# A mixture-of-experts trunk: where the kept expert rows are weighted and added, VectorE or GpSimd

## Chip, core and metric

The kernel runs on one core of a Trainium2 chip. The metric is device time in microseconds for one execution of the whole program; lower is better.

## What is computed

Two decoder layers on 256 tokens of width 1024 in fp32, then a final RMSNorm. The second layer ends in a mixture of eight SwiGLU experts, of which each token uses two. That part matters here:

```python
def _moe(x, router, wg, wu, wd):
    logits = (x @ router).astype(jnp.float32)
    top_val, top_idx = lax.top_k(logits, TOP_K)
    top_w = jax.nn.softmax(top_val, axis=-1)
    gate = jnp.sum(jax.nn.one_hot(top_idx, N_EXPERTS, dtype=jnp.float32) * top_w[..., None], axis=-2)
    y = jnp.zeros_like(x)
    for e in range(N_EXPERTS):
        y = y + gate[..., e:e + 1].astype(x.dtype) * _swiglu(x, wg[e], wu[e], wd[e])
    return y
```

D_MODEL is 1024, an expert is 3584 wide, and the result is added to the residual `h`.

## The kernel before

Every engine has its own program, written out by hand; semaphores join them. There is no scheduler: each engine runs its instructions in the order of the code.

**Weights.** A product in fp32 is made of three matmuls on parts of the operands. A weight tile of 2 MB lies in one of seven ring slots (`ring_a`, `ring_b`) and is taken in four quanta of 128x1024. For each quantum ScalarE copies it, rounded, to `w_hi` (L806), VectorE subtracts to get the rest, `w_lo` (L1416), and TensorE runs six matmuls on it (`three`, L1546 to L1548). `w_hi` and `w_lo` have four slots (NQ), so ScalarE and VectorE can be at most four quanta ahead of TensorE: a slot is refilled when TensorE signals `q_used`. VectorE's L1416 reads two SBUF operands, a ring slot and `w_hi`.

**Experts.** The loop over experts ("items" 0 to 7) has seven blocks f of 512 hidden columns. Each block takes a gate tile, an up tile and a down tile, so an item has 84 quanta. Beside them VectorE does two things for a block, both with one operand in PSUM: the product of the activated gate with up, called `mul` below (L1485), and the rest of the transposed hidden block, `hT_lo` (L1474). TensorE transposes the hidden block at L2067.

**Kept rows.** Tokens are gathered by expert. The outputs of experts 0 to 6 are stored in DRAM rows `xs`. While the last expert (item 7) runs, GpSimd's queue gathers each token's stored rows back with indirect DMAs into `tokens` (128 x 2 x 1024): first the one choice (n=0, two DMAs, t=0 and 1), later the other (n=1). `gate_kept`, worked out in `kept_gates` at the beginning of the expert stage, holds their weights. VectorE adds weight times row to `h` in four instructions (`kept_rows`, L1435), one behind the `mul` of each of the blocks f = 3, 4, 5 and 6. The second gather overwrites `tokens`, so it waits for the first two additions (`kept_added`).

**End.** Behind the last quanta TensorE scatters the last expert's rows (L2125, L2126), VectorE adds them to `h` (L1450), and the final norm and two stores of the output follow.

Of the kernel before, what the change touches and what calls it, by code (L numbers as in the profile page):

```python
# [11 lines left out]
ALU = mybir.AluOpType  # L12
ACT = mybir.ActivationFunctionType
AX = mybir.AxisListType
# [4 lines left out]
T = S // P  # L19
# [10 lines left out]
NE, FE = 8, 3584  # L30
# [59 lines left out]
def trunk(nc, A, consts_d, bands_d, out):  # L90
# [64 lines left out]
    AHEAD = 2 * NQ  # L155
# [4 lines left out]
    fills, n = {}, 0  # L160
# [5 lines left out]
    GCOLS, n = {}, 0  # L166
# [14 lines left out]
    with ExitStack() as ctx:  # L181
# [3 lines left out]
        def sem(name):  # L185
            return ctx.enter_context(nc.semaphore(name))
# [5 lines left out]
        h = sbuf("h", [T, D])  # L192
# [11 lines left out]
        tokens = sbuf("tokens", [T, D])  # L204
# [8 lines left out]
        gate_kept = sbuf("gate_kept", [T, 2])  # L213
# [51 lines left out]
        valid = sbuf("valid", [T, ITEMS], on=route)  # L265
# [38 lines left out]
        def slot(s):  # L304
# [26 lines left out]
            "logits_done", "top_done", "top_exp", "sel_done", "routed"))  # L331
        rwg_done = sem("rwg_done")
        xn_done = sem("xn_done")
        zeroed, xs_cleared, rows_done, xs_in, xg_loaded = map(sem, (
            "zeroed", "xs_cleared", "rows_done", "xs_in", "xg_loaded"))
        y_out, y_stored, kept_in, kept_added = map(sem, ("y_out", "y_stored", "kept_in", "kept_added"))
# [109 lines left out]
        @block.gpsimd  # L446
        def _(pool):
            def gains(*parts):
                at = 0
                for v, w in parts:  # L450
                    pool.dma_start(gain[:, at:at + w], v.partition_broadcast(P)).then_inc(gain_in, 16)
                    at += w
            pool.wait_ge(loaded[0], 16)
            pool.dma_start(sgu_w[:, :, :], A["sgu_w"][0].rearrange("g p q -> p g q")).then_inc(even_in, 16)
            gains((A["sgu_ln_g"][0], 512), (A["sgu_ln_b"][0], 512))
            for n, v in enumerate(("lam_q1", "lam_k1", "lam_q2", "lam_k2")):
                pool.dma_start(lamv[:, n, :], A[v][0].partition_broadcast(P)).then_inc(even_in, 16)
            with nc.allow_non_contiguous_dma("512 words, once"):
                pool.dma_start(sgu_b[:, :], A["sgu_b"][0].rearrange("g p -> p g")).then_inc(even_in, 16)
            pool.dma_start(rw[:, :, :], A["router"][0].rearrange("(c p) n -> p c n", p=P)).then_inc(rw_in, 16)  # L460

            pool.wait_ge(even_in, 16 * 6)
            pool.affine_select(out=sgu_w[:, :, :], in_=sgu_w[:, :, :], compare_op=ALU.is_ge, fill=0.0, base=0,
                               pattern=[[0, 4], [-1, P]], channel_multiplier=1).then_inc(sgu_masked, 1)

            pool.wait_ge(gain_in, 16 * 2)
            pool.wait_ge(ln_ready, 1)
            for t in range(T):
                vg = proj[:, t, 2048:2560]
                pool.tensor_scalar(vg, vg, st("ROOT", t, 1), st("LNBIAS", t, 1), ALU.mult, ALU.add).then_inc(ln_step, 1)  # L470
                pool.wait_ge(ln_step, 2 * t + 1)
                pool.tensor_tensor(vg, vg, gain[:, 0:512], ALU.mult).then_inc(ln_step, 1)
                pool.wait_ge(ln_step, 2 * t + 2)
                pool.tensor_tensor(vg, vg, gain[:, 512:1024], ALU.add).then_inc(ln_applied, 1)
            pool.wait_ge(ln_applied, 2)
            gains((A["norm_ffn_odd"][0], D))
            pool.wait_ge(h_done, 2)
            pool.memset(zeros[:, :], 0.0).then_inc(zeroed, 1)
            pool.dma_start(bands, bands_d).then_inc(bands_in, 16)
            pool.dma_start(pool_w[:, :, :], A["pool_w"][0].rearrange("g c d -> c g d")).then_inc(odd_in, 16)  # L480
            with nc.allow_non_contiguous_dma("512 words, once"):
                pool.dma_start(pool_s[:, :], A["pool_scale"][0].rearrange("(g d) -> d g", d=P)).then_inc(odd_in, 16)
            pool.wait_ge(zeroed, 1)
            pool.dma_start(xs.rearrange("n p d -> p n d"), zeros[:, :].rearrange("p (u d) -> p u d", u=1).to_broadcast(
                [P, ITEMS + 1, D])).then_inc(xs_cleared, 16)
            pool.wait_ge(xn_done, T)
            gains((A["final_norm"], D))
            pool.wait_ge(xs_cleared, 16)
            pool.wait_ge(rows_done, 1)
            for t in range(T):  # L490
                for n in range(2):
                    pool.indirect_dma_start(xs.rearrange("n p d -> (n p) d"),
                                            bass.IndirectOffsetOnAxis(row_of[:, t, n:n + 1], 0), tokens[:, t, :],
                                            None).then_inc(xs_in, 16)
            pool.wait_ge(xs_in, 16 * 2 * T)
            pool.wait_ge(gathered, 1)
            pool.wait_ge(y_stored, 16 * (NE - 1) + 1)
            for n in range(2):
                if n:
                    pool.wait_ge(kept_added, T)  # L500
                for t in range(T):
                    pool.indirect_dma_start(tokens[:, t, :], None, xs.rearrange("n p d -> (n p) d"),
                                            bass.IndirectOffsetOnAxis(row_of[:, t, n:n + 1], 0)).then_inc(kept_in, 16)


        @block.scalar
# [397 lines left out]
        def _(dve):  # L904
            chain = [0]
            split = [0]
            v = nc.vector

            def link(ins):

                chain[0] += 1
                ins.then_inc(dve_chain, 1)
                dve.wait_ge(dve_chain, chain[0])
# [182 lines left out]
            for n in range(4):  # L1096
                lo_upto(b + n + 5)
                f = (1, 3, 5, 7)[n]
# [304 lines left out]
            def kept_gates():  # L1403

                kept = NE - 1
                for n in range(2):
                    link(v.tensor_tensor(valid[:, :, 0:kept], rows[:, :, 0:kept], row_f[:, :, n:n + 1].to_broadcast(
                        [P, T, kept]), ALU.is_equal))
                    link(v.tensor_tensor(valid[:, :, 0:kept], valid[:, :, 0:kept], gate_of[:, :, 0:kept], ALU.mult))
                    link(v.reduce_sum(gate_kept[:, :, n:n + 1], valid[:, :, 0:kept], AX.X))  # L1410

            def expert_rest(i, q):

# [11 lines left out]
            def gathered_rests(n):  # L1425
                dve.wait_ge(xg_head, n + 1)
                v.tensor_tensor(xg_lo[:, :, :], ps[:, 0:2, :].rearrange("p b (c s) -> p (b c) s", s=P),
                                xg_hi[:, :, :].bitcast(F32), ALU.subtract).then_inc(xg_rest, 1)

            def kept_rows(n, t):  # L1430

                dve.wait_ge(kept_in, 16 * T * (n + 1))
                if n:
                    dve.wait_ge(kept_added, T)
                v.scalar_tensor_tensor(out=h[:, t, :], in0=tokens[:, t, :], scalar=gate_kept[:, t, n:n + 1], in1=h[:, t, :],  # L1435
                                       op0=ALU.mult, op1=ALU.add).then_inc(kept_added, 1)

            def y_rests(n, half):

# [17 lines left out]
                dve.wait_ge(last_added, after)  # L1457
                v.tensor_tensor(xn[:, 1, cols], h[:, 1, cols], gain[:, cols], ALU.mult).then_inc(scale_ready, 1)

            def item_rests(i, start, by_product, kept=False):  # L1460

                done = [start]

                def rests_upto(n):
                    while done[0] < n:
                        expert_rest(i, done[0])
                        done[0] += 1

                def rests_ahead(unit):
                    rests_upto(min(4 * (pos_of[unit] + 1) + NQ - 1, QI))  # L1470

                def hT_rests(f):
                    dve.wait_ge(hT_head, FB * i + f + 1)
                    v.tensor_tensor(hT_lo[:, f % 2], ps[:, 7, :].rearrange("p (c s) -> p c s", c=4),  # L1474
                                    hT_hi[:, f % 2].bitcast(F32), ALU.subtract).then_inc(hT_rest, 1)

                for f in range(FB):
                    if f:
                        rests_ahead(("gate", f))
                        hT_rests(f - 1)  # L1480
                    rests_ahead(("up", f))
                    dve.wait_ge(silu_done, FB * i + f + 1)
                    if f:
                        dve.wait_ge(hT_ready, FB * i + f)
                    v.tensor_tensor(g_mul, g_act, ps[:, 2 * (f % 2) + 1, :], ALU.mult).then_inc(mul_done, 1)  # L1485
                    if by_product and f == 0:
                        choose(i)
                    if kept and f >= 3:
                        kept_rows((f - 3) // 2, (f - 3) % 2)
                rests_upto(QI - 3)  # L1490
                hT_rests(FB - 1)
                if not by_product:
                    rests_upto(QI)
                    gathered_rests(i + 1)
                    rests_upto(QI + AHEAD)
                else:
                    rests_upto(QI)
# [11 lines left out]
            kept_gates()  # L1509
            with dve.Fori(0, NE - 1) as i:  # L1510
                item_rests(i, AHEAD, False)
            item_rests(NE - 1, AHEAD, True, kept=True)
            extra_count = dve.value_load(active[0:1, 0:1], min_val=0, max_val=EXTRA)
            with dve.Fori(NE, ITEMS) as i:
                with dve.If(extra_count + NE - i > 0):
# [656 lines left out]
```

## Time and profile before

| | us |
|---|---|
| median of 3 runs (1393.93 to 1394.96) | 1394.62 |
| profiled execution, device time | 1394.02 |
| its span, first to last instruction | 1391.9 |
| outside the span (1394.02 - 1391.9) | 2.1 |
| TensorE matmul busy | 1365.2 |
| VectorE busy | 1140.3 |
| ScalarE busy | 1006.8 |
| GpSimd busy | 31.2 |

The profile is of one execution. Times in it count from the start of its span. TensorE's matmuls are pipelined: the profile gives each some 0.39 us, but they follow one another every 0.23 us, so starts are better than busy time for telling whether TensorE waited. A VectorE instruction's time overlaps the next one's start by some 0.1 us.

### The profile page before, as it was taken

The page shows a single profiled execution, that of the slowest core. Times are in us where ns is not written, and L with a number is a line of the kernel's source. Part 1 is how long each engine was busy: PE and PEld are TensorE (multiplying, and loading weights), DVE is VectorE, ACT ScalarE, POOL GpSimd, SP SyncE. Part 2 cuts the span into 40 slices and gives each one's busy share as a digit, 9 for nine tenths or more (in the row PEclk, how much of TensorE's full clock was granted, in tenths as well). Part 3 has the DMA queues.
Part 4 walks back from the last instruction along what each step waited for, and adds up shares of the span by engine and source line. Part 5 has one row for each costly group of instructions (what it writes and reads, how often), then busy time and mean ns, then how long its engine had stood idle before and what let it go on. Part 6 is the DMA issues. An engine that isn't in the chain of part 4 may idle for free.

```text
span 1391.9 us, 19106 instructions
## 1 busy us (share of the span) xinstructions
PE 1365.2 (98%) x6794; PEld 1135.1 (82%) x6794; DVE 1140.3 (82%) x1197; ACT 1006.8 (72%) x1180; POOL 31.2 (2%) x35
## 2 busy tenths in 40 slices
PE   8999999999999999999999999999999999999996
PEld 7779989988787888888888888888888888888884
DVE  5676655556569999999999999999999989999996
ACT  5665544457548778778877877887787788788775
POOL 1201000000001000000000000000000000000010
PEclk9999999999999999999999999999999999999999
DMA  9467754354479999999999999999999999999960
GB/s 332 164 205 283 281 183 158 133 185 140 163 280 370 393 381 364 390 372 361 385 380 370 357 394 376 365 381 382 366 360 392 365 371 383 377 361 386 386 249 32
DMA packets 180619, 436.93 MB, mean 314 GB/s; under 512 B 4070, under 2 KB 8332, under 8 KB 180572
## 3 DMA queue, kind: packets, MB, share of 16 engines
q1 hardware_dynamic: 176816, 422.74, 82.7%
q0 software_dynamic: 3680, 13.54, 2.7%
q8 instruction: 30, 0.49, 0.1%
q14 instruction: 17, 0.14, 0.0%
q10 hardware_dynamic: 76, 0.02, 0.0%
HBM read 423.18 MB, written 13.11 MB: 313 GB/s over the span
## 4 chain that ended last, share of the span: by engine, by line
PE 91%; DVE 5%; ACT 3%; issue 1%; DMA 0%; SPq 0%; DVEq 0%; ACTq 0%
PE ps L1546 26%; PE ps L1547 26%; PE ps L1548 26%; PE ps L1801 3%; PE ps L1803 3%; PE ps L1802 3%; PE ps L2067 2%; DVE w_lo L922 1%; ACT w_hi L530 1%; DVE w_lo L1416 1%; DVE xt_lo L961 0%; PE ps L1573 0%; PE ps L2041 0%; ACT e L585 0%; DMA h<-in_x 0%
## 5 line engine op out<-in xcount | busy, mean ns | idle before, releaser
L1416 DVE TENSOR_TENSOR w_lo<-ring_a,w_hi 128x1024 fp32r<-128x1024 f32 x384 | 460.0, 1223 | 40.2 <-ACT w_hi L806 30.4
L806 ACT ACTIVATE w_hi<-ring_a 128x1024 fp32r<-128x1024 f32 x384 | 399.9, 1059 | 70.8 <-PE ps L1548 70.7
L1416 DVE TENSOR_TENSOR w_lo<-ring_b,w_hi 128x1024 fp32r<-128x1024 f32 x288 | 345.5, 1224 | 27.5 <-ACT w_hi L806 24.5
L1546 PE MATMUL ps<-w_hi,xg_hi 128*128 128x512 f32 x896 | 356.6, 398 | 2.1 <-DVE w_lo L1416 1.1
L1547 PE MATMUL ps<-w_lo,xg_hi 128*128 128x512 f32 x896 | 353.0, 394 | 0.0
L1548 PE MATMUL ps<-w_hi,xg_lo 128*128 128x512 f32 x896 | 351.6, 392 | 0.0
L806 ACT ACTIVATE w_hi<-ring_b 128x1024 fp32r<-128x1024 f32 x288 | 300.7, 1058 | 54.9 <-PE ps L1548 54.9
L922 DVE TENSOR_TENSOR w_lo<-ring_a,w_hi 128x1024 fp32r<-128x1024 f32 (+2 forms) x119 | 141.7, 1198 | 115.8 <-ACT w_hi L530 115.8
L530 ACT ACTIVATE w_hi<-ring_a 128x1024 fp32r<-128x1024 f32 (+2 forms) x119 | 121.9, 1033 | 130.1 <-PE ps L1803 65.2
L1546 PEld LDWEIGHTS ps<-w_hi,xg_hi 128*128 128x128 f32 x896 | 168.4, 188 | 41.8 <-DVE w_lo L1416 3.1
L1548 PEld LDWEIGHTS ps<-w_hi,xg_lo 128*128 128x128 f32 x896 | 168.3, 188 | 38.0
L1547 PEld LDWEIGHTS ps<-w_lo,xg_hi 128*128 128x128 f32 x896 | 168.4, 188 | 36.0
L1546 PE MATMUL ps<-w_hi,hT_hi 128*128 128x512 f32 x448 | 177.7, 397 | 0.5 <-DVE w_lo L1416 0.3
L1547 PE MATMUL ps<-w_lo,hT_hi 128*128 128x512 f32 x448 | 176.6, 394 | 0.0
L1548 PE MATMUL ps<-w_hi,hT_lo 128*128 128x512 f32 x448 | 175.9, 393 | 0.0
L1546 PEld LDWEIGHTS ps<-w_hi,hT_hi 128*128 128x128 f32 x448 | 84.1, 188 | 21.4 <-DVE w_lo L1416 2.5
L1548 PEld LDWEIGHTS ps<-w_hi,hT_lo 128*128 128x128 f32 x448 | 84.1, 188 | 19.1
L1801 PE MATMUL ps<-xt_hi,w_hi 128*128 128x256 f32 x352 | 99.0, 281 | 0.6 <-DVE xt_lo L961 0.4
L1547 PEld LDWEIGHTS ps<-w_lo,hT_hi 128*128 128x128 f32 x448 | 84.1, 188 | 18.4
L1803 PE MATMUL ps<-xt_hi,w_lo 128*128 128x256 f32 x352 | 98.4, 280 | 0.0
L1802 PE MATMUL ps<-xt_lo,w_hi 128*128 128x256 f32 x352 | 98.4, 279 | 0.0
L1546 PE MATMUL ps<-w_hi,xt_hi 128*128 128x512 f32 (+2 forms) x176 | 69.7, 396 | 0.6 <-DVE xt_lo L961 0.6
(322 smaller groups left out, 1339.8 us busy)
## 6 DMA issues: line engine op xcount, KB each, us to landing
ring_a<-in_moe_wg SPq DMA_DIRECT2D x40, 2048.0 KB, 9.4
ring_a<-in_moe_wu SPq DMA_DIRECT2D x32, 2048.0 KB, 10.0
ring_b<-in_moe_wd SPq DMA_DIRECT2D x32, 2048.0 KB, 9.3
ring_b<-in_moe_wu SPq DMA_DIRECT2D x24, 2048.0 KB, 9.5
ring_a<-in_moe_wd SPq DMA_DIRECT2D x24, 2048.0 KB, 9.2
ring_b<-in_moe_wg SPq DMA_DIRECT2D x16, 2048.0 KB, 11.4
ring_a<-in_ffn_wg SPq DMA_DIRECT2D x5, 2048.0 KB, 9.2
ring_a<-in_ffn_wu SPq DMA_DIRECT2D x5, 2048.0 KB, 7.9
```

The source lines that it names most:

```text
L530: copy(w_hi[:, q % NQ, 0:w], slot(u % RING1)[:, k * w:(k + 1) * w], ACT.Copy).then_inc(hi_done, 1)
L806: nc.scalar.activation(w_hi[:, (Q1 + q) % NQ, 0:1024], slot(j % RING2)[:, 1024 * k:1024 * k + 1024], ACT.Copy).then_inc(hi_done, 1)
L922: v.tensor_tensor(w_lo[:, q % NQ, 0:w], slot(u % RING1)[:, k * w:(k + 1) * w], w_hi[:, q % NQ, 0:w].bitcast(F32), ALU.subtract).then_inc(l ...
L1416: v.tensor_tensor(w_lo[:, (Q1 + q) % NQ, 0:1024], slot(j % RING2)[:, 1024 * k:1024 * k + 1024], w_hi[:, (Q1 + q) % NQ, 0:1024].bitcast(F32 ...
L1546: pe.matmul(out_, a_hi, w_hi[:, q, c0:c1], start=first, stop=False)
L1547: pe.matmul(out_, a_hi, w_lo[:, q, c0:c1], start=False, stop=False)
L1548: return pe.matmul(out_, a_lo, w_hi[:, q, c0:c1], start=False, stop=last)
L1801: pe.matmul(o, w_hi[:, q % NQ, a:b], xt_hi[:, kc, :], start=(kc == 0), stop=False)
L1802: pe.matmul(o, w_hi[:, q % NQ, a:b], xt_lo[:, kc, :], start=False, stop=False)
L1803: ins = pe.matmul(o, w_lo[:, q % NQ, a:b], xt_hi[:, kc, :], start=False, stop=(kc == KC - 1))
L2067: ins = pe.transpose(ps[:, 7, P * c:P * (c + 1)], g_mul[:, P * c:P * (c + 1)], ident)
```

## The change

GpSimd takes over the four weighted additions. Behind each pair of gathers it scales the two 128x1024 halves of `tokens` in place by `gate_kept` (two TENSOR_SCALAR), then adds each to `h` (two TENSOR_TENSOR). VectorE's `kept_rows` is gone; in its place VectorE waits once, behind the last item's quanta, until all four additions are done. `kept_gates` signals GpSimd when the weights are there.

```diff
             for n in range(2):
-                if n:
-                    pool.wait_ge(kept_added, T)
                 for t in range(T):
                     pool.indirect_dma_start(tokens[:, t, :], None, xs.rearrange("n p d -> (n p) d"),
                                             bass.IndirectOffsetOnAxis(row_of[:, t, n:n + 1], 0)).then_inc(kept_in, 16)
+                pool.wait_ge(kept_in, 16 * T * (n + 1))
+                if n == 0:
+                    pool.wait_ge(kept_weighted, 1)
+                for t in range(T):
+                    nc.gpsimd.tensor_scalar(tokens[:, t, :], tokens[:, t, :], gate_kept[:, t, n:n + 1], 0.0, ALU.mult,
+                                            ALU.add).then_inc(kept_scaled, 1)
+                for t in range(T):
+                    pool.wait_ge(kept_scaled, T * n + t + 1)
+                    nc.gpsimd.tensor_tensor(h[:, t, :], h[:, t, :], tokens[:, t, :], ALU.add).then_inc(kept_added, 1)
+                pool.wait_ge(kept_added, T * (n + 1))
...
-                    link(v.reduce_sum(gate_kept[:, :, n:n + 1], valid[:, :, 0:kept], AX.X))
+                    ins = v.reduce_sum(gate_kept[:, :, n:n + 1], valid[:, :, 0:kept], AX.X)
+                    if n == 0:
+                        link(ins)
+                ins.then_inc(kept_weighted, 1)
...
-            def kept_rows(n, t):
-
-                dve.wait_ge(kept_in, 16 * T * (n + 1))
-                if n:
-                    dve.wait_ge(kept_added, T)
-                v.scalar_tensor_tensor(out=h[:, t, :], in0=tokens[:, t, :], scalar=gate_kept[:, t, n:n + 1], in1=h[:, t, :],
-                                       op0=ALU.mult, op1=ALU.add).then_inc(kept_added, 1)
...
-                    if kept and f >= 3:
-                        kept_rows((f - 3) // 2, (f - 3) % 2)
...
-            item_rests(NE - 1, AHEAD, True, kept=True)
+            item_rests(NE - 1, AHEAD, True)
+            dve.wait_ge(kept_added, 2 * T)
             extra_count = dve.value_load(active[0:1, 0:1], min_val=0, max_val=EXTRA)
```

GpSimd's queue at its end, before: the four gathers L502, the third waiting for VectorE's additions.

```order
L502 DMA tokens<-xs,row_of 128x1024 [waits y_stored,gathered,xs_in]
L502 DMA tokens<-xs,row_of 128x1024
L502 DMA tokens<-xs,row_of 128x1024 [waits kept_added]
L502 DMA tokens<-xs,row_of 128x1024
L181 UNCONDITIONAL_BRANCH
```

And in the changed kernel:

```order
L501 DMA tokens<-xs,row_of 128x1024 [waits y_stored,gathered,xs_in]
L501 DMA tokens<-xs,row_of 128x1024
L507 TENSOR_SCALAR tokens<-tokens,gate_kept 128x1024 [waits kept_weighted,kept_in]
L507 TENSOR_SCALAR tokens<-tokens,gate_kept 128x1024
L511 TENSOR_TENSOR h<-h,tokens 128x1024 [waits kept_scaled] x2
L501 DMA tokens<-xs,row_of 128x1024 [waits kept_added]
L501 DMA tokens<-xs,row_of 128x1024
L507 TENSOR_SCALAR tokens<-tokens,gate_kept 128x1024 [waits kept_in]
L507 TENSOR_SCALAR tokens<-tokens,gate_kept 128x1024
L511 TENSOR_TENSOR h<-h,tokens 128x1024 [waits kept_scaled] x2
L181 UNCONDITIONAL_BRANCH [waits kept_added]
```

Eight GpSimd instructions on 128x1024 have joined the gathers, and the third gather now waits for GpSimd's own additions.

VectorE's queue in the last two blocks of the last item, before (L1416 is a quantum's `w_lo`, L1485 the `mul`, L1474 `hT_lo`, L1435 a kept row, L1513 reads the count of extra items):

```order
L1485 TENSOR_TENSOR xn<-xn,ps 128x512 [waits hT_ready,silu_done]
L1435 SCALAR_TENSOR_TENSOR h<-tokens,gate_kept,h 128x1024 [waits kept_added,kept_in]
L1416 TENSOR_TENSOR w_lo<-ring_a,w_hi 128x1024 [waits hi_done] x5
L1416 TENSOR_TENSOR w_lo<-ring_b,w_hi 128x1024 [waits hi_done] x3
L1474 TENSOR_TENSOR hT_lo<-ps,hT_hi 128x512 [waits hT_head]
L1416 TENSOR_TENSOR w_lo<-ring_b,w_hi 128x1024 [waits hi_done] x4
L1485 TENSOR_TENSOR xn<-xn,ps 128x512 [waits hT_ready,silu_done]
L1435 SCALAR_TENSOR_TENSOR h<-tokens,gate_kept,h 128x1024 [waits kept_added,kept_in]
L1416 TENSOR_TENSOR w_lo<-ring_b,w_hi 128x1024 [waits hi_done] x2
L1474 TENSOR_TENSOR hT_lo<-ps,hT_hi 128x512 [waits hT_head]
L1416 TENSOR_TENSOR w_lo<-ring_b,w_hi 128x1024 [waits hi_done] x3
L1513 TENSOR_LOAD active
```

The same stretch in the changed kernel, whose lines have moved (L1428 is `w_lo`, L1489 `mul`, L1478 `hT_lo`, L1516 the count):

```order
L1489 TENSOR_TENSOR xn<-xn,ps 128x512 [waits hT_ready,silu_done]
L1428 TENSOR_TENSOR w_lo<-ring_a,w_hi 128x1024 [waits hi_done] x5
L1428 TENSOR_TENSOR w_lo<-ring_b,w_hi 128x1024 [waits hi_done] x3
L1478 TENSOR_TENSOR hT_lo<-ps,hT_hi 128x512 [waits hT_head]
L1428 TENSOR_TENSOR w_lo<-ring_b,w_hi 128x1024 [waits hi_done] x4
L1489 TENSOR_TENSOR xn<-xn,ps 128x512 [waits hT_ready,silu_done]
L1428 TENSOR_TENSOR w_lo<-ring_b,w_hi 128x1024 [waits hi_done] x2
L1478 TENSOR_TENSOR hT_lo<-ps,hT_hi 128x512 [waits hT_head]
L1428 TENSOR_TENSOR w_lo<-ring_b,w_hi 128x1024 [waits hi_done] x3
L1516 TENSOR_LOAD active [waits kept_added]
```

Four kept rows are gone (two of them in this piece), and the count waits for GpSimd. Nothing else moves on VectorE; TensorE, ScalarE and SyncE keep their order.

## Rows read from the trace of the kernel before

**Rows 1.** Windows: busy time of each engine, an inner stretch and the last item.

```profile
core 0: us, PE busy (x) PEld busy (x) DVE busy (x) ACT busy (x) POOL busy (x), PEclk, DMA share, GB/s
1030.00:1150.00 120.00, 120.00 (x540) 97.78 (x539) 110.01 (x100) 97.78 (x104) 0.00 (x0) 1.00 1.01 373
1254.00:1374.00 120.00, 119.70 (x533) 96.49 (x532) 112.84 (x105) 95.13 (x101) 6.63 (x4) 1.00 0.78 292
```

**Rows 2.** Timeline of TensorE around the first kept row.

```profile
1315.00 0.40 PE L1546 MATMUL ps<-w_hi,hT_hi 128*128 128x512 f32 x1
...
1316.39 0.39 PE L1546 MATMUL ps<-w_hi,hT_hi 128*128 128x512 f32 x1
...
1318.47 0.46 PE L1546 MATMUL ps<-w_hi,hT_hi 128*128 128x512 f32 x1
1318.77 0.39 PE L1547 MATMUL ps<-w_lo,hT_hi 128*128 128x512 f32 x1
```

**Rows 3.** Timeline of VectorE in the last item, steady and around the first kept row.

```profile
1286.76 1.23 DVE L1416 TENSOR_TENSOR w_lo<-ring_b,w_hi 128x1024 fp32r<-128x1024 f32 x1 [0.15 <-ACT w_hi L806]
...
1315.36 0.68 DVE L1485 TENSOR_TENSOR xn<-xn,ps 128x512 f32<-128x512 f32 x1
1315.96 1.28 DVE L1435 SCALAR_TENSOR_TENSOR h<-tokens,gate_kept,h 128x1024 f32<-128x1024 f32 x1
1317.15 1.22 DVE L1416 TENSOR_TENSOR w_lo<-ring_a,w_hi 128x1024 fp32r<-128x1024 f32 x1
1318.29 6.93 DVE L1416 TENSOR_TENSOR w_lo<-ring_b,w_hi 128x1024 fp32r<-128x1024 f32 x6
```

**Rows 4.** Waits in 1250 to 1392: who for whom, total, times, longest.

```profile
ACT w_hi L806 <- PE ps L1548: 17.0, 53, 0.7
DVE w_lo L1416 <- ACT w_hi L806: 5.7, 28, 0.4
PEld ps L1546 <- DVE w_lo L1416: 2.5, 6, 0.6
```

**Rows 5.** Timeline of the end of the last item, all engines.

```profile
1367.36 1.28 DVE L1435 SCALAR_TENSOR_TENSOR h<-tokens,gate_kept,h 128x1024 f32<-128x1024 f32 x1
1369.12 0.60 ACT L848 ACTIVATE hT_hi<-ps 128x512 fp32r<-128x512 f32 x1 [0.69 <-PE ps L2067]
1370.83 0.68 DVE L1474 TENSOR_TENSOR hT_lo<-ps,hT_hi 128x512 fp32r<-128x512 f32 x1
1371.43 3.48 DVE L1416 TENSOR_TENSOR w_lo<-ring_b,w_hi 128x1024 fp32r<-128x1024 f32 x3
1371.91 1.06 ACT L806 ACTIVATE w_hi<-ring_b 128x1024 fp32r<-128x1024 f32 x1 [0.30 <-PE ps L1548]
1374.96 0.50 PE L1546 MATMUL ps<-w_hi,hT_hi 128*128 128x512 f32 x1 [0.18 <-DVE w_lo L1416]
```

**Rows 6.** Timeline of GpSimd: a small memset, and the even layer's norm.

```profile
0.30 0.10 POOL L2163 MEMSET const-float32-0.0<- 128x1 f32 x1 [0.30 <-issue]
59.42 0.77 POOL L470 TENSOR_SCALAR proj<-proj,stats 128x512 f32<-128x512 f32 x1 [33.53 <-DVE stats L1109]
60.27 1.30 POOL L472 TENSOR_TENSOR proj<-proj,gain 128x512 f32<-128x512 f32 x1
61.66 1.27 POOL L474 TENSOR_TENSOR proj<-proj,gain 128x512 f32<-128x512 f32 x1
62.92 1.74 POOL L470 TENSOR_SCALAR proj<-proj,stats 128x512 f32<-128x512 f32 x1
```

**Rows 7.** Timeline of VectorE beside that norm.

```profile
57.73 1.22 DVE L922 TENSOR_TENSOR w_lo<-ring_a,w_hi 128x1024 fp32r<-128x1024 f32 x1
60.13 0.68 DVE L1030 SCALAR_TENSOR_TENSOR e<-ps,table 128x512 f32<-128x512 f32 x1
61.98 2.03 DVE L922 TENSOR_TENSOR w_lo<-ring_a,w_hi 128x1024 fp32r<-128x1024 f32 x1
```

**Rows 8.** Timeline of GpSimd in the last item: the gathers.

```profile
1278.53 1.98 POOL L502 DMA_INDIRECT tokens<-xs,row_of  x1 [0.30 <-issue]
1334.64 1.68 POOL L502 DMA_INDIRECT tokens<-xs,row_of  x1 [54.13 <-DVE h L1435]
1336.63 1.97 POOL L502 DMA_INDIRECT tokens<-xs,row_of  x1 [0.30 <-issue]
```

**Rows 9.** Issues of DMAs, 1250 to 1392: size, median us to landing.

```profile
tokens<-xs,row_of POOLq DMA_INDIRECT x4, 9.6
```

**Rows 10.** Windows at the very end: busy time and granted clock.

```profile
1380.00:1382.00 2.00, 0.81 (x4) 0.67 (x4) 1.74 (x3) 1.50 (x5) 0.00 (x0) 1.00 0.00 0
1384.00:1385.00 1.00, 0.00 (x0) 0.00 (x0) 0.88 (x3) 0.58 (x2) 0.00 (x0) 1.00 0.00 0
1385.00:1386.00 1.00, 0.00 (x0) 0.00 (x0) 0.71 (x2) 0.75 (x2) 0.00 (x0) 0.70 0.00 0
```

More of the change, by code:

```diff
@@ L333, in trunk @@
         xn_done = sem("xn_done")
+        kept_scaled, kept_weighted = sem("kept_scaled"), sem("kept_weighted")
         zeroed, xs_cleared, rows_done, xs_in, xg_loaded = map(sem, (
@@ L1458, in with_gain, with item_rests @@
                 v.tensor_tensor(xn[:, 1, cols], h[:, 1, cols], gain[:, cols], ALU.mult).then_inc(scale_ready, 1)
-            def item_rests(i, start, by_product, kept=False):
+            def item_rests(i, start, by_product):
                 done = [start]
```

## Prediction

> **What bounds the kernel now.** I read the windows first. In an inner stretch of the experts TensorE is busy for all 120 us, and in the last item for 119.70 of 120 [rows 1]. Matmul busy time flatters, so I checked the starts: a quantum of six matmuls takes 1316.39 - 1315.00 = 1.39 us, and these starts follow without a hole [rows 2]. TensorE is the bound, and a microsecond in which it stands still is a microsecond of the result.
>
> VectorE comes next: busy 110.01 of the same 120 us [rows 1]. Back to back its quanta take 6.93 / 6 = 1.155 us [rows 3], against TensorE's 1.39, so it gains 0.235 us on TensorE with each. A block has 12 quanta and two instructions with a PSUM operand, `mul` and `hT_lo`, at some 0.6 us from start to start (1315.36 to 1315.96) [rows 3]: 12 x 1.155 + 1.2 = 15.1 us, while TensorE needs at least 12 x 1.39 = 16.7 us.
>
> The waits say how the two are coupled. ScalarE waits for TensorE 53 times, VectorE for ScalarE 28 times, TensorE's weight loads for VectorE only 6 times, 2.5 us in all [rows 4]. VectorE is ahead, held back by the four slots of `w_hi` and `w_lo`. What matters is how much delay this lead swallows. The kernel does that experiment itself: the first kept row holds VectorE for 1317.15 - 1315.96 = 1.19 us right behind a `mul` [rows 3], and the only trace of it on TensorE is one pitch of 1318.77 - 1318.47 = 0.30 us where 0.23 is normal [rows 2]. So the lead there is 1.19 - 0.07 = 1.1 us. Before a `mul` it is that plus its 0.6, 1.7 us. I take 1.4 us for an instruction that falls anywhere.
>
> **What the removal gives.** Four kept rows leave VectorE. Three of them lie in the body of the item, in places like the one above, at 0.07 us each: 0.2 us. The fourth is different. It runs at 1367.36, and with it gone everything behind it can move up. `hT_lo` started at 1370.83, though its ScalarE half was there at 1369.12 + 0.60 = 1369.72; the three last quanta follow, and TensorE's last wait for one ends at 1374.96 [rows 5]. Without the kept row `hT_lo` could start near 1369.8, but the last quantum's `w_hi` is there only at 1371.91 + 1.06 = 1372.97 [rows 5]; plus 0.15 us to get going [rows 3] and 1.155 gives 1374.3, which is 0.6 to 0.7 us earlier than 1374.96. So the removal gives 0.2 + 0.6 = 0.8 us; its bounds are 0 and 0.2 + 1.2 = 1.4 us. The wait that replaces the four lies behind the last quantum, where VectorE next needs the last expert's output.
>
> **What the addition costs.** GpSimd gets four scalings and four additions on 128x1024. The trace has both at half the size, beside other work: scaling 0.77 us, addition 1.30 us [rows 6]. A memset of one element takes 0.10 us [rows 6]; with that as the fixed part, the full size is 2 x 0.77 - 0.10 = 1.44 us and 2 x 1.30 - 0.10 = 2.50 us. Two of each: 7.9 us for a batch; plain doubling gives 8.3.
>
> If that ran freely beside VectorE, it would cost nothing. It doesn't seem to. VectorE's `w_lo` takes 1.22 us at 57.73. At 61.98, with GpSimd's addition of 61.66 under way, the same shape takes 2.03 us. GpSimd's addition ends at 61.66 + 1.27 = 62.93; VectorE then needs 1.1 more, which ends at 64.0, as the row does. And GpSimd's next scaling, sent off at 62.92, takes 1.74 instead of 0.77 us: it waited for VectorE until about 63.9 [rows 6, 7]. Yet a VectorE instruction with one operand in PSUM kept its 0.68 us at 60.13 beside such work [rows 7]. I read this as exclusion: `w_lo`, with two SBUF operands, and a GpSimd instruction that reads SBUF don't run together, and the one that comes second waits until the first is done. The Trainium skill has this as a rule (SBUF — State Buffer, Who interferes with whom): a VectorE instruction with two SBUF inputs contends with GpSimd instructions that read SBUF, and the second to issue is blocked for the whole of the first. By that rule, the trace agrees, the change is a loss.
>
> How often do they collide? 84 of VectorE's instructions in the item are `w_lo`, and it is hardly ever idle. So each of GpSimd's instructions holds VectorE up. A batch then goes in turns: GpSimd, one `w_lo`, GpSimd, one `w_lo`, and so on, as at 61.66 to 64.66 [rows 6, 7], where VectorE, waiting, got in ahead of GpSimd's next instruction. The account of a batch:
> - VectorE is shut out for 7.9 us.
> - `mul` or `hT_lo` can run meanwhile: four quanta carry 4/12 of a block's 1.2 us, so 0.4 us off.
> - The lead takes 1.4 us.
> - Four `w_lo` in between gain 4 x 0.235 = 0.9 us.
> - TensorE stands still for 7.9 - 0.4 - 1.4 - 0.9 = 5.2 us.
>
> The second batch is like the first, if the lead has grown back. GpSimd sends two gathers, 1336.63 - 1334.64 = 2.0 us apart [rows 8], and the second lands 9.6 us later [rows 9]: 11.6 us. In 17.2 us (120/7, a block with its transposes) VectorE has 17.2 - 15.1 = 2.1 us to spare, so in 11.6 us 1.4 us: the lead is whole again. Two batches: 10.4 us.
>
> Both unknowns have two ends. At the low one the lead is 1.7, a `mul` and an `hT_lo` hide 1.2 and five quanta gain 1.2: 3.8 us a batch, 7.6 in all, less 1.4: +6.2. At the high one a batch holds 8.3, hides nothing, has the lead of 1.1 and gains three quanta, 0.7: 6.5, so +13.0 with nothing given back. I stay in the middle, because nothing ties the batch to a place in the block.
>
> The sum: +10.4 - 0.8 = **+9.6 us**. The profiled execution would take 1394.02 + 9.6 = 1403.6 us; the median of the runs shown is 0.6 us above it, 1394.62, so I predict 1404.2 us (1400.8 to 1407.6 for this case).
>
> The Trainium skill (GPSIMD Engine Reference, Performance versus the Vector engine) gives 4497 ns for an addition on 2048 elements. Half of that, an estimate of 2.25 us, would make the four additions 1.0 us shorter than in my sum.
>
> **What hides the rest.** The gathers are as many as before. The second pair moves from 1334.64 to about 1302 (1278.53 + 9.6 = 1288, plus 7.9 and four to five `w_lo`), into a time when the DMA engines are full. It brings no new bytes, and no TensorE or ScalarE wait for a load stands among the waits of this stretch [rows 4]. If this cover were thin, 1 MB at 373 GB/s [rows 1] is 2.8 us. The missing semaphore in `kept_gates` and the new one cost an instruction or nothing. `kept_weighted` is long satisfied. All of GpSimd's work should be over by about 1325, 50 us before VectorE asks for it.
>
> **Rivals.**
> 1. *GpSimd waits politely* (chance 0.23). VectorE running back to back might keep GpSimd out until it pauses of itself, for ScalarE [rows 3] or with a `mul`. Each GpSimd instruction then finds a full lead. A scaling of 1.44 us costs nothing; an addition of 2.50 costs 2.50 - 1.4 = 1.1, or 0.5 if it starts with a `mul`: 2.0 to 4.4 us for four, less 0.8: +1.2 to +3.6, so 1395.8 to 1398.2. For it: VectorE starts its next instruction before the last one's time is over. Against it: at 62.93 the waiting one got in at once. A page speaks against it too: the Trainium skill (VectorE: DVE Perf Modes, The DRAIN you can't avoid) says that VectorE's pipe empties between two instructions; no row here shows it.
> 2. *No contention in this place* (0.07). The long `w_lo` was something else, and only the gain is left: 1394.62 - 0.8 = 1393.8.
> 3. *Faster* (0.02). VectorE's load is TensorE's limit in the whole item, so that all four kept rows return in full: 4 x 1.19 = 4.8 us, 1389.8. It decides if TensorE's waits behind kept rows are larger than their rows show: above 0.7 us each, where I read 0.07 [rows 2].
> 4. *The clock falls* (0.05). In a batch TensorE has 1.39 us of work in each 1.44 + 1.155 = 2.6 or 2.50 + 1.155 = 3.7 us. At the very end it had 0.81 us in two and kept the granted clock of 1.00, the level of 2.4 GHz, and still did with nothing at all in 1384 to 1385; only then the clock fell [rows 10]. If it fell in the batches and stayed down from the one to the other, some 15 us at half speed cost 15 more: about 1419.
> 5. *GpSimd is starved and comes late* (0.04). Work left when VectorE goes idle at 1374.9 is paid in full: a whole batch, 7.9 us, in place of the stalls, gives 1394.62 + 7.9 - 0.8 = 1401.7, and with the second gather, 11.6 more, 1413. It begins to count if 28 us of work (two batches and a gather) stretch to 87, from 1288 to 1375.
>
> **Chances.** The forecast has 0.59. A measurement here can tell about 0.2%, 2.8 us. Above 1397.4 lie the forecast, rivals 4 and 5, and a little under half of rival 1: 0.59 + 0.05 + 0.04 + 0.09 = 0.77. Within 0.2% lie rival 2 and the rest of rival 1: 0.07 + 0.14 = 0.21. Faster has 0.02. The range leaves out rivals 2 and 3 below and 4 and most of 5 above, and reaches from 1395.0 to 1408.0.
>
> **What would show it.** Four TENSOR_SCALAR and four TENSOR_TENSOR on GpSimd, the first near 1290, each stretched by up to 1.2 us if it waits for a `w_lo`. Beside them seven or eight `w_lo` of 2.5 to 3.7 us where all others take 1.22. TensorE's loads waiting for `w_lo` for some 10 us more in two clusters, near 1290 to 1302 and 1313 to 1325; nothing different before 1288; the last wait of TensorE at the end 0.6 us shorter. I am wrong if `w_lo` keeps 1.22 us throughout (rival 2), or if it is stretched but GpSimd's batch spreads over much more than 12 us (rival 1 or 5).

## Result: 1399.79 us against 1394.32 us

The changed kernel takes 1399.79 us (median of 6 runs, 1398.58 to 1401.69); the kernel before 1394.32 us (6 runs, 1393.93 to 1394.96). The ratio is 1.0043, with a 95% interval of 1.0032 to 1.0053: 5.5 us slower. The forecast was 1404.2 us, range 1395.0 to 1408.0. The direction and the mechanism were right, the size was too large: +5.5 us where +9.6 was forecast, and 1.0 us below the narrower bounds given for this case (1400.8 to 1407.6). The time alone would not have decided it, since it lies between these bounds and those of rival 1 (1395.8 to 1398.2); the traces do.

The profiled execution of the changed kernel has a span of 1398.1 us against 1391.9. Its page begins:

```profile
span 1398.1 us, 19110 instructions
...
PE 1366.2 (98%) x6794; PEld 1135.3 (81%) x6794; DVE 1146.2 (82%) x1193; ACT 1007.0 (72%) x1180; POOL 52.5 (4%) x43
```

VectorE has four instructions fewer, 5.1 us of work, and yet is "busy" 5.9 us longer than before (1140.3). What is stretched shows in the groups of 1250 to 1398 (lines: group, shapes, count, busy us, mean ns, idle before):

```profile
L1428 DVE TENSOR_TENSOR w_lo<-ring_a,w_hi 128x1024 fp32r<-128x1024 f32 x48 | 67.0, 1425 | 3.8 <-ACT w_hi L815 2.6
L1428 DVE TENSOR_TENSOR w_lo<-ring_b,w_hi 128x1024 fp32r<-128x1024 f32 x39 | 47.4, 1248 | 3.1 <-ACT w_hi L815 2.8
L1489 DVE TENSOR_TENSOR xn<-xn,ps 128x512 f32<-128x512 f32 x7 | 4.8, 679 | 0.0
```

`w_lo` from `ring_a` has a mean of 1425 ns, where one took 1.22 us [rows 3]; `mul`, with an operand in PSUM, keeps 679 ns. The timeline of GpSimd in the last item, one instruction a row as far as narrow windows part them:

```profile
1289.85 1.87 POOL L507 TENSOR_SCALAR tokens<-tokens,gate_kept 128x1024 f32<-128x1024 f32 x1 [7.98 <-DMA tokens<-xs,row_of]
1291.71 2.07 POOL L507 TENSOR_SCALAR tokens<-tokens,gate_kept 128x1024 f32<-128x1024 f32 x1
1293.75 3.38 POOL L511 TENSOR_TENSOR h<-h,tokens 128x1024 f32<-128x1024 f32 x1
1297.10 3.36 POOL L511 TENSOR_TENSOR h<-h,tokens 128x1024 f32<-128x1024 f32 x1
...
1300.73 1.68 POOL L501 DMA_INDIRECT tokens<-xs,row_of  x1 [0.27 <-POOL h L511]
...
1310.30 4.24 POOL L507 TENSOR_SCALAR tokens<-tokens,gate_kept 128x1024 f32<-128x1024 f32 x2 [6.63 <-DMA tokens<-xs,row_of]
1314.51 6.71 POOL L511 TENSOR_TENSOR h<-h,tokens 128x1024 f32<-128x1024 f32 x2
```

And VectorE beside the first batch:

```profile
1288.18 2.55 DVE L1428 TENSOR_TENSOR w_lo<-ring_b,w_hi 128x1024 fp32r<-128x1024 f32 x2 [0.23 <-ACT w_hi L815]
1290.89 1.90 DVE L1428 TENSOR_TENSOR w_lo<-ring_b,w_hi 128x1024 fp32r<-128x1024 f32 x1 [0.16 <-ACT w_hi L815]
1292.71 0.68 DVE L1478 TENSOR_TENSOR hT_lo<-ps,hT_hi 128x512 fp32r<-128x512 f32 x1
1293.31 1.54 DVE L1428 TENSOR_TENSOR w_lo<-ring_b,w_hi 128x1024 fp32r<-128x1024 f32 x1
1294.78 3.44 DVE L1428 TENSOR_TENSOR w_lo<-ring_a,w_hi 128x1024 fp32r<-128x1024 f32 x1
...
1298.14 3.40 DVE L1428 TENSOR_TENSOR w_lo<-ring_a,w_hi 128x1024 fp32r<-128x1024 f32 x1
```

Read side by side, the two take turns; a time in which a `w_lo` waits for GpSimd is called a hold below. GpSimd's first scaling waits for the `w_lo` that ends near 1290.7, and runs to 1291.72. The next `w_lo` waits for it: 1.90 us, 0.68 more than 1.22. The second scaling waits for that one, and runs under `hT_lo`, which keeps its 0.68 us; the `w_lo` behind takes 1.54 us. The first addition (1293.75) waits for a `w_lo` until 1294.85 and runs until 1297.13, 2.28 us of its own; the `w_lo` issued at 1294.78 takes 3.44 us. Then once more. The waits of 1286 to 1325 show the other end of it:

```profile
PE ps L1549 <- DVE w_lo L1428: 5.7, 4, 1.6
```

TensorE's matmuls wait for `w_lo` four times, twice in each batch. In the kernel before, in the same stretch, all that TensorE waited for VectorE was this, of a weight load:

```profile
PEld ps L1546 <- DVE w_lo L1416: 0.2, 1, 0.2
```

For a finer measure than the device time I use the last item alone: from the start of block 0's `mul` to the start of VectorE's last instruction. Before it takes 1385.45 - 1269.45 = 116.00 us, changed 1392.03 - 1269.41 = 122.62 us: +6.62. This leaves out what has nothing to do with the change: in the nine profiles the item begins at 1269.35 to 1269.97, and from the start of its last instruction to the end of the span, the store of the output above all, it takes 5.7 to 6.7 us. Up to the `mul` of block 1 all nine agree (11.54 us), so a difference of a few tenths in the item is read as real here, though it rests on one profile each. The cost lies where the two batches are: from block 0's `mul` to block 4's it is 1339.30 - 1269.41 = 69.89 us against 1332.49 - 1269.45 = 63.04, +6.85.

### The profile page after: what moved, and what is told of

Read it like the earlier page. It is cut to its first block, busy times and chain, and to the rows that moved or that the text cites. A ratio compares the mean times of both kernels' runs of the same rounds, so it can differ in the third digit from the quotient of the medians.

```text
span 1398.1 us, 19110 instructions
## 1 busy us (share of the span) xinstructions
PE 1366.2 (98%) x6794; PEld 1135.3 (81%) x6794; DVE 1146.2 (82%) x1193; ACT 1007.0 (72%) x1180; POOL 52.5 (4%) x43
## 4 chain that ended last, share of the span: by engine, by line
PE 90%; DVE 6%; ACT 3%; issue 1%; DMA 0%; ACTq 0%; DVEq 0%
PE ps L1549 26%; PE ps L1550 25%; PE ps L1551 25%; PE ps L1804 3%; PE ps L1806 3%; PE ps L1805 3%; PE ps L2070 2%; DVE w_lo L1428 2%; DVE w_lo L931 1%; ACT w_hi L539 1%; DVE xt_lo L970 0%; PE ps L1576 0%; PE ps L2044 0%; ACT e L594 0%; PE ps L1559 0%
## 5 line engine op out<-in xcount | busy, mean ns | idle before, releaser
L1428 DVE TENSOR_TENSOR w_lo<-ring_a,w_hi 128x1024 fp32r<-128x1024 f32 x384 | 469.6, 1248 | 39.8 <-ACT w_hi L815 29.9
L1428 DVE TENSOR_TENSOR w_lo<-ring_b,w_hi 128x1024 fp32r<-128x1024 f32 x288 | 346.6, 1227 | 28.0 <-ACT w_hi L815 25.8
## 6 DMA issues: line engine op xcount, KB each, us to landing
ring_a<-in_moe_wu SPq DMA_DIRECT2D x32, 2048.0 KB, 10.1
```

The source lines that it names most:

```text
L1428: v.tensor_tensor(w_lo[:, (Q1 + q) % NQ, 0:1024], slot(j % RING2)[:, 1024 * k:1024 * k + 1024], w_hi[:, (Q1 + q) % NQ, 0:1024].bitcast(F32 ...
```

## Experiments

Four kernels were compared on one chip with 33 runs of the kernel before (median 1394.15), three on another with 22 (1394.31). The column "item" is the measure just described, from one profile each.

| kernel | median us | ratio to before, 95% | item us | to before |
|---|---|---|---|---|
| changed kernel | 1399.79 | 1.0043 (1.0032 to 1.0053) | 122.62 | +6.62 |
| no rows | 1393.08 | 0.9994 (0.9985 to 1.0003) | 115.71 | -0.29 |
| write only | 1393.79 | 0.9997 (0.9988 to 1.0006) | 115.69 | -0.31 |
| scale only | 1394.75 | 1.0005 (0.9996 to 1.0014) | 116.86 | +0.86 |
| pieces | 1398.83 | 1.0029 (1.0017 to 1.0042) | 120.74 | +4.74 |
| spaced | 1394.26 | 1.0000 (0.9991 to 1.0009) | 116.82 | +0.82 |
| early rows on VectorE | 1394.20 | 1.0001 (0.9992 to 1.0010) | 116.01 | +0.01 |
| early rows and early count | 1393.89 | 0.9997 (0.9988 to 1.0006) | 115.87 | -0.13 |

**No rows: the removal alone.** Nobody adds the kept rows.

```diff
-                (GpSimd's two tensor_scalar and two tensor_tensor, their waits)
-            dve.wait_ge(kept_added, 2 * T)
+            dve.wait_ge(kept_in, 16 * T * 2)
```

> The changed kernel without GpSimd's eight instructions, so that nobody adds the kept rows (the first seven experts are missing from the output); the gathers run one pair behind the other. Exclusion theory (a w_lo and a GpSimd instruction that reads SBUF don't run together): only the gain of the removal is left, 0.4 to 0.8 us, so 1393.5 to 1393.9 against 1394.3 before, and every w_lo of the last item takes 1.22 us. Rival (the second gather, now early, collides with the weight loads and costs the time): the kernel stays well above before, 1397 or more, with ScalarE waiting for loads.

Measured 1393.08, a little below the expected 1393.5 to 1393.9, and every `w_lo` of 1280 to 1345 took 1217 to 1228 ns (count, then shortest, median and longest):

```profile
L1419 DVE TENSOR_TENSOR w_lo<-ring_a,w_hi x24: 1217/1226/1228, 1294.3 to 1344.6; 128x1024 fp32r<-128x1024 f32 x24
L1419 DVE TENSOR_TENSOR w_lo<-ring_b,w_hi x22: 1218/1226/1227, 1279.8 to 1333.0; 128x1024 fp32r<-128x1024 f32 x22
```

So the gain of taking the work off VectorE is 0.3 us in the item and 1.1 us (not told apart from none) in the medians. The second pair of gathers went out at 1287.76, earlier than in the changed kernel, and cost nothing: the rival with the gathers falls.

**Write only: as much GpSimd work, but no reads.**

```diff
+                for k in range(7):
+                    ...
+                    pool.memset(tokens[:, k % 2, :], 0.0).then_inc(kept_scaled, 1)
```

in place of the scalings and additions, so that here too the kept rows are missing from the output.

> The changed kernel with GpSimd's eight instructions replaced by fourteen memsets of 128x1024 on the same tile, 0.95 us each, 13.3 us in all, as much as the 13.1 us that the eight hold VectorE up (kept rows are not added). They only write. Exclusion theory: no w_lo is stretched, 1393.5 to 1393.9 as without the rows. Rival (any GpSimd work beside VectorE slows it): some 7 us more, about 1400.

Measured 1393.79, the same as no rows within the intervals. GpSimd's and VectorE's groups in 1250 to 1392:

```profile
L507 POOL MEMSET tokens<- 128x1024 f32 x14 | 12.7, 962 | 16.3 <-DMA tokens<-xs,row_of 16.3
...
L1424 DVE TENSOR_TENSOR w_lo<-ring_a,w_hi 128x1024 fp32r<-128x1024 f32 x48 | 57.7, 1224 | 5.5 <-ACT w_hi L811 4.5
```

12.7 us of memsets beside VectorE, and `w_lo` stays at 1224 ns. It is not GpSimd's activity that holds VectorE up. The one thing that the eight instructions do and the memsets don't, beside arithmetic, is to read SBUF. No run has GpSimd read without arithmetic, so the two are told apart only by the rule cited in the prediction.

**Scale only: the four scalings on GpSimd, the additions on VectorE.**

```diff
+                for t in range(T):
+                    nc.gpsimd.tensor_scalar(tokens[:, t, :], tokens[:, t, :], gate_kept[:, t, n:n + 1], 0.0, ALU.mult,
+                                            ALU.add).then_inc(kept_scaled, 1)
...
-                v.scalar_tensor_tensor(out=h[:, t, :], in0=tokens[:, t, :], scalar=gate_kept[:, t, n:n + 1], in1=h[:, t, :],
-                                       op0=ALU.mult, op1=ALU.add).then_inc(kept_added, 1)
+                v.tensor_tensor(h[:, t, :], h[:, t, :], tokens[:, t, :], ALU.add).then_inc(kept_added, 1)
```

> GpSimd scales the four gathered halves, VectorE adds them in the places of the kernel before with a plain addition. Theory of the lead (TensorE stands still only for what a hold exceeds VectorE's lead of 1.1 to 1.7 us, plus what follows before it has grown back): two holds of 1.03 us in a row, with one w_lo between, just about use up the lead, 0 to 0.8 us a batch: 1394.3 to 1396. Rival (the stall is proportional to the time that GpSimd works, 4.1 of 13.1 us of the changed kernel's 6.9): 1396.5.

Measured 1394.75, inside what the lead allows, and +0.86 us in the item. All of it falls into the second batch. The first pair of scalings stretches two `w_lo` by 0.68 and 0.32 us and costs nothing: from block 0's `mul` to block 4's it takes 62.98 us, as in no rows (62.97). That is a hold of 1.0 us swallowed whole by the lead. In the second batch VectorE is held up by a scaling (one `w_lo` takes 0.61 us more) and by a wait that neither theory had named: the second scaling is done late, and VectorE's third addition waits for it. How much of the 0.86 us each of them is worth was not told apart.

```profile
1350.42 0.68 DVE L1494 TENSOR_TENSOR xn<-xn,ps 128x512 f32<-128x512 f32 x1
1351.53 1.23 DVE L1445 TENSOR_TENSOR h<-h,tokens 128x1024 f32<-128x1024 f32 x1 [0.43 <-POOL tokens L509]
```

The proportional rival, 1396.5, lies above the interval (1.0014 is 1396.1), but not by much. With scale only at +0.86 and the whole change at +6.62, the scalings by themselves cost little. That the additions cost nearly all the rest is argued: no run has the additions alone.

**Pieces: the same work in halves, back to back.**

```diff
+                    for s in range(2):
+                        cols = slice(512 * s, 512 * s + 512)
+                        nc.gpsimd.tensor_scalar(tokens[:, t, cols], tokens[:, t, cols], gate_kept[:, t, n:n + 1], 0.0,
+                                                ALU.mult, ALU.add).then_inc(kept_scaled, 1)
```

and the additions likewise.

> The changed kernel with each of GpSimd's eight instructions cut in two of 512 columns, back to back: sixteen. The lead account: the holds are together as long or a little longer (13 to 15 us), but twice as many w_lo run between them and each gains 0.235 us, 1.9 us instead of 0.9 in a batch: 1 us less stall a batch, so about 2 us less than the changed kernel, 1398; the w_lo are stretched to 1.7 to 2.4 us instead of 3.4. Rival (only the sum of the holds counts): 1399.8 or slower.

Measured 1398.83. In the item it is 1.9 us less than the changed kernel, as the account has it; in the medians 1.0 us, which the intervals don't tell from none. The longest `w_lo` was 2320 ns where it had been 3441. But the expectation had the holds as long as before or longer, and they were shorter: what all stretched `w_lo` have above 1.22 us adds up to 9.7 us here and to 10.8 in the changed kernel. So 1.1 of the 1.9 us can be the shorter hold, and pieces says little for the lead by itself.

**Spaced: the same halves, one every two or three quanta.**

```diff
+                        pool.wait_ge(lo_done, Q1 + QI * (NE - 1) + 28 + 30 * n + 2 * (2 * t + s))
                         nc.gpsimd.tensor_scalar(...)
...
+                        pool.wait_ge(lo_done, Q1 + QI * (NE - 1) + 36 + 30 * n + 3 * (2 * t + s))
                         nc.gpsimd.tensor_tensor(...)
```

> The same sixteen half instructions, but each waits until VectorE has reached a certain quantum of the last item: one each two quanta for the scalings, one each three for the additions, and they end by quantum 77 of 84. The lead account: a hold of 0.5 to 0.8 us is swallowed, one of 1.2 us against 0.5 to 0.7 us regained in three quanta uses up the lead by the end of a batch, 0.5 to 1.5 us a batch. So 1394.5 to 1396.5. Rival (the sum of the holds counts): 1399.8, as in the changed kernel.

Measured 1394.26, ratio 1.0000. That is below the expected 1394.5 to 1396.5. The sixteen instructions are those of pieces, and still hold `w_lo` up, to 2321 ns at most and by 8.4 us in all; but TensorE's waits of 1280 to 1345 are all but gone. For `w_lo` in this stretch, who waited for it:

```profile
  PEld ps L1556: 0.4, 1
```

In pieces that answer reads:

```profile
  PEld ps L1554: 6.1, 8
  PE ps L1554: 2.8, 5
```

The spaced instructions run on until 1364, and in the rest, 1345 to 1380, the weight loads wait 1.9 us in 3 times; the kernel before has 2.0 us in 4 times there (the matmuls 0.6 us against 0.3). Against no rows, pieces costs 5.0 us in the item for a hold of 9.7, spaced 1.1 us for 8.4. So it isn't the sum of the holds that costs, but what of them exceeds the lead before it has grown back. Of all results this speaks most directly for the lead account.

**Early rows on VectorE, and early count.**

```diff
-                    if kept and f >= 3:
-                        kept_rows((f - 3) // 2, (f - 3) % 2)
+                    if kept and 2 <= f < 6:
+                        kept_rows((f - 2) // 2, (f - 2) % 2)
```

> The kernel before with VectorE's four kept rows one block earlier, behind the mul of blocks 2 to 5 instead of 3 to 6. The fourth leaves the end. The gain of the removal is that of the fourth row: 0.4 to 0.6 us, 1393.7 to 1393.9, with TensorE's last wait for w_lo 0.6 us shorter. Rival (the second gather lands too late for block 4, whose mul comes near 1332): VectorE waits at the third row and the gain is lost or turned into a loss of 1 us or more.

Measured 1394.20 and +0.01 us in the item: not the expected gain of 0.4 to 0.6 us, and no late gather either (the third row ran at 1333.58, right behind its `mul`). In the end of the item everything went as forecast up to the last `w_lo`, and no further. The end of early rows:

```profile
1371.20 3.53 DVE L1416 TENSOR_TENSOR w_lo<-ring_b,w_hi 128x1024 fp32r<-128x1024 f32 x3 [0.25 <-ACT w_hi L806]
1372.41 1.06 ACT L806 ACTIVATE w_hi<-ring_b 128x1024 fp32r<-128x1024 f32 x1 [0.29 <-PE ps L1548]
1375.37 1.28 ACT L892 ACT_TABLE_LOAD   x1 [1.90 <-issue]
...
1376.77 0.58 ACT L830 ACTIVATE y_hi<-ps 128x512 fp32r<-128x512 f32 x1
1377.39 0.69 DVE L1441 TENSOR_TENSOR y_lo<-ps,y_hi 128x512 fp32r<-128x512 f32 x1 [2.65 <-ACT y_hi L830]
```

The last `w_lo` ends 1374.73 - 1367.27 = 7.5 us behind the last `mul`; before it was 1374.91 - 1366.76 = 8.2 [rows 5]. But `y_lo` begins 1377.39 - 1367.27 = 10.1 us behind it, as before (1376.88 - 1366.76). VectorE stands idle for 2.65 us instead of 1.98: it waits for ScalarE's `y_hi`, which follows a table load that comes 1.90 us behind ScalarE's last `w_hi`. The 0.7 us gained on VectorE turned into a longer wait for ScalarE. The changed kernel and no rows show the same 2.65 us.

The last kernel tries that chain: the kernel with early rows, with ScalarE's read of the count moved ahead of the last item.

```diff
+            act.wait_ge(routed, 1)
+            extra_count = act.value_load(active[0:1, 0:1], min_val=0, max_val=EXTRA)
             item_heads(NE - 1, AHEAD, True)
-            act.wait_ge(routed, 1)
-            extra_count = act.value_load(active[0:1, 0:1], min_val=0, max_val=EXTRA)
```

> The kernel with VectorE's kept rows one block earlier, and ScalarE reads the count of extra items ahead of the last item instead of behind it. In the changed kernel's trace ScalarE's table load ends after TensorE has the first half of the last output ready, so that 0.2 to 0.4 us of the tail's gain are lost. If that reading holds, the table load starts up to 1.9 us earlier and the kernel takes 0.3 to 0.5 us less than with early rows alone: 1393.2 to 1393.6. If the 1.9 us belong to the loop's branches and not to the read, nothing changes, 1393.8.

The gap shrank from 1.90 to 1.11 us:

```profile
1374.34 1.28 ACT L892 ACT_TABLE_LOAD   x1 [1.11 <-issue]
...
1375.74 0.58 ACT L830 ACTIVATE y_hi<-ps 128x512 fp32r<-128x512 f32 x1
1377.02 0.69 DVE L1441 TENSOR_TENSOR y_lo<-ps,y_hi 128x512 fp32r<-128x512 f32 x1 [2.53 <-ACT y_hi L830]
```

The item gained 0.14 us on early rows, not the expected 0.3 to 0.5; the medians, from two chips, differ by 0.3 us and can't be told apart. `y_hi` was there at 1376.32, and VectorE began only at 1377.02. The wait is put down to `y_hi`, but the chain of work of 1373 to 1379 names another: VectorE's own queue, which reads the count (L1513) and walks through the loop over the extra items (L1514, L1515), where nothing is to be done. It ends like this (DVEq is that queue; start, length):

```profile
1376.43 0.06 DVEq L1515
...
1376.75 0.05 DVEq L1514
...
1376.92 0.05 DVEq L1440
1376.97 0.05 issue
1377.02 0.70 DVE y_lo L1441
```

From the last `mul` to the end of L1440 these steps take 1376.97 - 1367.03 = 9.94 us, and in the kernel before as much, 1376.70 - 1366.76, where `y_hi` came 0.15 us later still. So ScalarE's table load was the last wait, and VectorE's empty loop stands 0.15 us behind it: that is what early count could gain.

## Why the prediction came out as it did

**What bounds the kernel: right.** TensorE's waits for `w_lo` came out as time: the matmuls' four waits have 5.7 us by the profile, which models where a matmul ends, and block 4's `mul` comes 6.85 us later. The item took 6.6 us more, the span 6.2.

**That reading GpSimd instructions and `w_lo` exclude each other: right.** The changed kernel's rows show the turns, write only shows that GpSimd instructions that only write are not enough, and `mul` and `hT_lo`, with their PSUM operand, kept their 0.68 us. In what excludes what, that is also the rule of the Trainium skill (SBUF — State Buffer, Who interferes with whom), down to the exception for instructions that only write; by that rule, the traces agree. The prediction's other half of it, that the second to issue is the one blocked, does not hold throughout: in pieces a GpSimd scaling let a `w_lo` pass that was issued 1.1 us behind it (last section). Eight `w_lo` were stretched, as foreseen, but only four of them to the 2.5 to 3.7 us of the prediction, the other four to 1.54 and 1.9.

**Size of a batch: the term that was mis-sized.** I had GpSimd shut VectorE out for 7.9 us, from 1.44 us for a scaling and 2.50 for an addition. In the first batch the scaling took 1.0 us (1290.7 to 1291.72) and the addition 2.28, so 6.6 us, below even the low end of my bounds, which left the 7.9 as it was. The fixed part of 0.10 us was not at fault; taking an instruction's whole time for a hold was. In spaced, halves with 512 columns ran both free and behind a `w_lo`:

```profile
1340.10 0.70 POOL L510 TENSOR_SCALAR tokens<-tokens,gate_kept 128x512 f32<-128x512 f32 x1 [1.16 <-DVE w_lo L1435]
1337.15 1.22 DVE L1435 TENSOR_TENSOR w_lo<-ring_a,w_hi 128x1024 fp32r<-128x1024 f32 x1 [0.16 <-ACT w_hi L822]
1337.17 1.77 POOL L510 TENSOR_SCALAR tokens<-tokens,gate_kept 128x512 f32<-128x512 f32 x1 [11.35 <-DVE w_lo L1435]
...
1310.19 1.31 POOL L517 TENSOR_TENSOR h<-h,tokens 128x512 f32<-128x512 f32 x1 [2.36 <-DVE w_lo L1435]
1305.46 1.23 DVE L1435 TENSOR_TENSOR w_lo<-ring_a,w_hi 128x1024 fp32r<-128x1024 f32 x1
1305.59 2.24 POOL L517 TENSOR_TENSOR h<-h,tokens 128x512 f32<-128x512 f32 x1 [1.22 <-DVE w_lo L1435]
```

Free, a half scaling takes 0.70 us; behind the `w_lo` that ends at 1338.37 it needs only 1338.94 - 1338.37 = 0.57. A half addition takes 1.31 us free, and 1307.83 - 1306.69 = 1.14 behind a `w_lo`. So some 0.15 us of each instruction pass while it waits. Doubled, less the same 0.10, 0.57 and 1.14 give 1.04 and 2.18 us, close to the 1.0 and 2.28 measured at full size. Rows 6 and 7 held this already: the scaling of 62.92 ended at 64.66, 0.65 us behind the `w_lo`, where I took 0.77. The estimate from the Trainium skill (GPSIMD Engine Reference, Performance versus the Vector engine), 2.25 us for an addition, was nearer than mine. Of the 6.6 us more was hidden than the 0.4 I had taken: the sum of what the four `w_lo` were stretched by is 0.68 + 0.32 + 2.22 + 2.18 = 5.4 us, since the second scaling ran under `hT_lo` and the first began in a pause of VectorE. That both batches met an `hT_lo` is luck; nothing in the change ties them to it. Forecast for this line: 7.5.

**The lead and what is regained: right in size, as far as can be told.** No rows puts the removal at -0.29, so the eight instructions cost 6.62 + 0.29 = 6.9 us, 3.45 a batch. What is left, 5.4 - 3.45 = 1.95 us, is what the lead and the regained time together swallowed; I had 1.4 + 0.9 = 2.3. The two were not measured apart. Of the 3.5 us by which the forecast's 10.4 for the two batches was too high, the stretches make 2 x 7.5 - 2 x 5.4 = 4.2; the 1.95 in place of 2.3 takes 0.7 back.

**The gain of the removal: 0.3 us, not 0.8.** The three rows in the body were worth 0.2 us, as read: from block 0's `mul` to block 6's, no rows takes 1366.43 - 1269.35 = 97.08 us, before 97.31. The end was not, though TensorE's last wait for `w_lo` did end 0.7 us earlier. I followed VectorE's and TensorE's chain to the last `w_lo` and stopped there. From block 6's `mul` to the last instruction it takes 18.69 us before, 18.63 in the changed kernel. ScalarE's chain to `y_hi` was next in line, with VectorE's own empty loop 0.15 us behind; the trace of before has both (the table load at 1374.87, `y_hi` at 1376.27).

**Rivals.** GpSimd waiting politely: wrong for the additions, which get in behind one `w_lo` each. For scalings there is something in it (last section). The last point against it, that VectorE's pipe empties between two instructions, carries nothing here: back to back `w_lo` start 1.155 us apart and take 1.22 each [rows 3], so they overlap. Contention absent, faster, the clock, starvation: none came. TensorE's granted clock stayed at 1.00, the level of 2.4 GHz, in each batch, though TensorE did little there; the window of 1300 to 1302 in the changed kernel, with 0.40 us of matmuls (the 1.00 near the end of the row is the clock):

```profile
1300.00:1302.00 2.00, 0.40 (x2) 0.36 (x3) 2.00 (x2) 1.06 (x1) 1.73 (x2) 1.00 1.05 412
```

## What to carry to other kernels

An engine with little work is no free helper where its instructions and those of the engine it is to relieve shut each other out. Here GpSimd needed 1.0 + 2.28 us, with VectorE's `w_lo` shut out, for what costs VectorE 1.28 us itself. Before moving work off an engine, measure what its removal alone can bring (here 0.3 us in the item) by leaving it out; it bounds the whole idea. And if such work must go there, cut it into pieces below the lead of the pipeline and space them: the same instructions went from +4.7 to +0.8 us. Even so it gained nothing here: left on VectorE, the four rows cost 0.3 us.

## What was not expected

In pieces, a GpSimd scaling let two `w_lo` pass, the second at its normal 1.22 us, before it got its turn:

```profile
1313.65 2.82 POOL L509 TENSOR_SCALAR tokens<-tokens,gate_kept 128x512 f32<-128x512 f32 x1 [6.46 <-DMA tokens<-xs,row_of]
1313.62 1.23 DVE L1433 TENSOR_TENSOR w_lo<-ring_a,w_hi 128x1024 fp32r<-128x1024 f32 x1 [0.26 <-ACT w_hi L820]
1314.77 1.22 DVE L1433 TENSOR_TENSOR w_lo<-ring_a,w_hi 128x1024 fp32r<-128x1024 f32 x1
```

It ended at 1313.65 + 2.82 = 1316.47, some 0.5 us behind the end of the second. In scale only the first scaling of the second batch behaved alike (3.13 us, issued at 1346.30, with `w_lo` undisturbed until 1348.5). Over the four traces with scalings there is a pattern. They got in behind the first `w_lo` where VectorE then paused or went on to `mul` or `hT_lo`, as all four did in the changed kernel. Where another `w_lo` stood ready, all but one (in spaced) let that pass too. The additions of the changed kernel got in behind one each even so. So who gets the next turn between back-to-back instructions isn't plain alternation, nor the order of issue. What decides it, no run here tells.
